# Expert rows by a one-hot product and in two bounded gathers: a decoder step on one core

## What is computed

```python
s = sigmoid(xt @ router_w)                    # 576 x 16 scores
# best of 4 groups by the sum of its two best scores, then the two best experts in that group
w = take(s, e_idx); w = w / sum(w)            # combine: 576 x 16, two entries a row
for e in range(N_EXPERTS):                    # 16 experts, D_EXPERT 512
    h = silu(xt @ e_wg[e]) * (xt @ e_wu[e])
    y = y + combine[:, e:e + 1] * (h @ e_wd[e])
x = layer_norm(DN_ALPHA * x + y, ln_g[2], ln_b[2])
```

## Time and profile before

| | us |
|---|---|
| median of 3 runs | 1470.54 |
| lowest, highest | 1467.07, 1470.69 |
| the profiled execution, its own time | 1473.95 |
| its span, first to last instruction | 1471.7 |

### The profile page before, as it was taken

One profiled execution on the slowest core, in us unless ns is written; L12 is line 12 of the kernel. 1 busy time (PEld: TensorE's weight loads), 2 busy tenths in 40 slices (PEclk: granted clock), 3 DMA queues, 4 the chain that ended last, 5 costly groups with the idle time before them and its releaser, 6 DMA issues.

```text
span 1471.7 us, 20300 instructions
## 1 busy us (share of the span) xinstructions
PE 1338.8 (91%) x8065; PEld 1170.1 (80%) x8065; DVE 788.7 (54%) x1068; ACT 535.5 (36%) x734; POOL 403.3 (27%) x306
## 2 busy tenths in 40 slices
PE   4997998989999888999999999887994999999985
PEld 4987998989888777989998877765883788888862
DVE  7137275572726577722321430322446799999936
ACT  1243421526221454111001011343103688788840
POOL 8464555545245233223332000011000000011010
PEclk9998999999999999999999999997995999999998
DMA  7553323322133212234336301246523899999933
GB/s 242 162 187 102 108 85 111 108 82 86 45 94 87 63 46 65 65 93 119 103 108 201 122 29 57 87 181 241 213 86 95 322 406 410 410 411 412 408 141 128
DMA packets 153498, 239.95 MB, mean 163 GB/s; under 512 B 6400, under 2 KB 111033, under 8 KB 145089
## 3 DMA queue, kind: packets, MB, share of 16 engines
q1 hardware_dynamic: 131472, 177.98, 34.6%
q0 software_dynamic: 14544, 51.52, 9.9%
q10 hardware_dynamic: 7393, 9.20, 1.9%
HBM read 214.08 MB, written 24.60 MB: 162 GB/s over the span
## 4 chain that ended last, share of the span: by engine, by line
PE 49%; DMA 3%; DVE 3%; issue 1%; ACT 1%; POOL 0%; DVEq 0%; POOLq 0%; SPq 0%; ACTq 0%
PE bank L1110 46%; DMA kv_k<-in_cache_mem_k_dram 2%; PE bank L1552 1%; PE bank L1437 1%; PE bank L1135 1%; DVE x_tok L2271 0%; PE bank L1560 0%; DMA yb<-expert_rows,ints 0%; DVE small L2261 0%; ACT kv_t L773 0%; DMA kv_v<-in_cache_mem_v_dram 0%; DMA xg<-x_scratch,table 0%; ACT pT L773 0%; DMA expert_rows<-y_out 0%; DVE expert_weights_lo L2045 0%
## 5 line engine op out<-in xcount | busy, mean ns | idle before, releaser
L2045 DVE TENSOR_TENSOR expert_weights_lo<-expert_weights,expert_weights_hi 128x2048 fp32r<-128x2048 f32 x96 | 218.5, 2290 | 34.5 <-ACT expert_weights_hi L1034 33.2
L1034 ACT ACTIVATE expert_weights_hi<-expert_weights 128x2048 fp32r<-128x2048 f32 x96 | 182.7, 1916 | 22.1 <-PE bank L1110 14.6
L1110 PE MATMUL bank<-x_hi,gate_weights_hi 128*128 128x288 f32 x512 | 163.8, 320 | 12.1 <-ACT gate L932 11.4
L1110 PE MATMUL bank<-x_hi,gate_weights_lo 128*128 128x288 f32 x512 | 152.2, 297 | 0.0
L1110 PE MATMUL bank<-x_lo,gate_weights_hi 128*128 128x288 f32 x512 | 152.1, 297 | 0.0
L1110 PE MATMUL bank<-x_hi,mixer_weights_hi 128*128 128x288 f32 x448 | 137.9, 308 | 0.9 <-ACT q_all L813 0.9
L1110 PE MATMUL bank<-ob,branch_weights 128*128 128x288 f32 (+1 forms) x512 | 134.5, 405 | 0.0
L1110 PE MATMUL bank<-x_lo,mixer_weights_hi 128*128 128x288 f32 x448 | 134.5, 300 | 0.0
L1110 PE MATMUL bank<-x_hi,mixer_weights_lo 128*128 128x288 f32 x448 | 134.3, 300 | 0.0
L2326 POOL TENSOR_TENSOR mixer_weights_lo<-mixer_weights,mixer_weights_hi 128x1024 fp32r<-128x1024 f32 x52 | 128.2, 2466 | 4.2
L932 ACT ACTIVATE gate<-bank,pc 128x288 f32<-128x288 f32 x64 | 31.7, 501 | 226.4 <-PE bank L1110 223.8
(11 more groups left out here) (418 smaller groups left out, 2914.9 us busy)
## 6 DMA issues: line engine op xcount, KB each, us to landing
expert_weights<-in_e_wg_dram SPq DMA_DIRECT2D x32, 1024.0 KB, 8.8
expert_weights<-in_e_wu_dram SPq DMA_DIRECT2D x32, 1024.0 KB, 9.1
expert_weights<-in_e_wd_dram SPq DMA_DIRECT2D x32, 1024.0 KB, 8.9
mixer_weights<-in_w_in_dram SPq DMA_DIRECT2D x36, 512.0 KB, 4.0
gate_weights<-in_w_in_dram SPq DMA_DIRECT2D x32, 512.0 KB, 4.1
branch_weights<-in_w_branch_dram SPq DMA_DIRECT2D x32, 256.0 KB, 3.7
kv_k<-in_cache_mem_k_dram POOLq DMA_DIRECT2D x8, 1024.0 KB, 7.5
kv_v<-in_cache_mem_v_dram POOLq DMA_DIRECT2D x8, 1024.0 KB, 5.5
```

The lines of the kernel that those rows point to most:

```text
L1034: act.activation(w_hi[n % HIS][:], w_raw[n % RAW][:], ACT.Copy).then_inc(w_hi_done, 1)
L1110: return pe.matmul(out, lhsT, rhs, start=start, stop=stop)
L2045: dve.tensor_tensor(w_lo[n % RAW][:], w_raw[n % RAW][:], w_hi[n % HIS][:].bitcast(F32), ALU.subtract).then_inc(w_lo_done, 1)
```

## The change

It has three parts.

**First expert.** Expert 0's turned rows come from a product of x_tok with a one-hot table on PE and no longer from a gather and turns. DVE builds the table first_hot (128 x 640) from the count product, ahead of the slot arithmetic. PE runs 2 x 4 x 5 f32 products of 128 x 128 before it waits for hot_row. On DVE, piece 2's low part moves from ahead of the slot arithmetic to behind the table; x0's low part (`rows_lo(0)`) moves from behind piece 3 to ahead of the table copy. POOL's first gathers are for experts 1 and 2.

**Two passes.** POOL gathers ya and yb twice, with a bound: rows of the first 14 experts (FIRST_PASS, 1792 rows) when expert 13's rows are stored, and the rest after expert 14's (yb) and expert 15's (ya) store. Indices outside a pass lie above its bound, which skips them. The ya tiles lie in other places, free earlier. Expert 15's rows are stored in two halves, each when its half is copied.

**Token rows.** ACT scales x_tok by ALPHA in place in the d steps of experts 0 to 4. DVE adds wb * yb to x_tok after both yb passes (`earlier_term`). PE's sum has then two products for each half, x_tok with the identity and ya with its diagonal, in the order first_terms 0, 1, 2, ya 0, first_terms 3, ya 1, 2, 3, first_terms 4, ya 4. The pair diagonals on DVE are one a tile instead of two and one.

```diff
@@ -477,9 +477,10 @@
-        ya = place("ya", 0, [P, NT, D])
+        ya = [place(f"ya{t}", at, [P, D]) for t, at in enumerate((49088, 50112, 51136, 11264, 40640))]
...
+        first_hot = place("first_hot", 14336, [P, NT, P])
@@ -629,6 +631,8 @@
+        rows_scaled, terms_added = sem("token_rows_scaled"), sem("earlier_terms_added")
+        FIRST_PASS = P * (NE - 2)
@@ -728,8 +732,14 @@
                     store_rows(pieces[before][1])
-            for e in range(NE - 3, NE):
+            for e in range(NE - 3, NE - 1):
                 store_rows(e)
+            e = NE - 1
+            for s, name in enumerate((f"eY{e}", f"eY'{e}")):
+                b, use = uses[name]
+                sp.wait_ge(free[b], use + 1)
+                half = slice(512 * s, 512 * s + 512)
+                sp.dma_start(ys_d[P * e:P * e + P, half], y_out[:, e % 2, half]).then_inc(ys_stored[e % 2], 16)
@@ -1068,6 +1078,10 @@
                         gated(0)
+                    if kind == "d" and part and e < NT:
+                        act.wait_ge(x2_stored, 16 * NT)
+                        rows = x_tok[0:TILES[e], e, :]
+                        act.activation(rows, rows, ACT.Copy, scale=ALPHA).then_inc(rows_scaled, 1)
                     if kind == "d":
@@ -1536,6 +1550,15 @@
+            pe.wait_ge(first_ready, 1)
+            for s in range(2):
+                ps, fu = acquire(pe, f"eX{chr(39) * s}0")
+                for a in range(4):
+                    for t in range(NT):
+                        rows = TILES[t]
+                        m = mm(ps[:, P * a:P * a + P], x_tok[0:rows, t, 4 * s + a:D:KD], first_hot[0:rows, t, :], t == 0, t == NT - 1)
+                m.then_inc(fu, 1)
             pe.wait_ge(hot_ready, 1)
@@ -1562,8 +1585,9 @@
                 if what == "x":
-                    pe.wait_ge(xg_landed[n % 2], 16 * (n // 2 + 1))
-                    turn_gathered(n, n % 2)
+                    if n:
+                        pe.wait_ge(xg_landed[n % 2], 16 * ((n + 1) // 2))
+                        turn_gathered(n, n % 2)
                 elif what == "h":
@@ -1612,35 +1636,32 @@
-                for t in range(NT):
-                    pe.wait_ge(yb_landed[t], 32)
-            pe.wait_ge(diag_ready, NT)
-            def scaled(t, s, n, rows_of_pair, start, stop):
+            def summed(t, s, weights, rows_of_pair, start, stop):
...
-                return mm(bank[sum_banks[t][s]][0:rows, :], pair_diag[0:rows, n, 0:rows],
+                return mm(bank[sum_banks[t][s]][0:rows, :], weights[0:rows, 0:rows],
...
-            def earlier_terms(t):
+            def first_terms(t):
...
-                pe.wait_ge(yb_landed[t], 16)
+                pe.wait_ge(terms_added, t + 1)
...
-                    scaled(t, s, 0, x_tok[:, t, :], True, False)
-                    scaled(t, s, 2 + 2 * t, yb[t][:], False, False)
-            for t in range(NT - 1):
-                earlier_terms(t)
+                    summed(t, s, cst[:, C_ID:C_ID + P], x_tok[:, t, :], True, False)
+            for t in range(3):
+                first_terms(t)
+            pe.wait_ge(diag_ready, NT)
...
-                    earlier_terms(t)
-                pe.wait_ge(ya_landed[t], 16)
+                    first_terms(t)
+                pe.wait_ge(ya_landed[t], 32)
...
-                    scaled(t, s, 1 + 2 * t, ya[:, t, :], False, True).then_inc(sum_full, 1)
+                    summed(t, s, pair_diag[:, t, :], ya[t][:], False, True).then_inc(sum_full, 1)
+                if t == 0:
+                    first_terms(3)
@@ -2138,9 +2159,13 @@
-            weights_lo(2)
             ps, fr = arrived(dve, "pos")
             placed, count = by(ps[:, 0:NT * NE], NE), ps[:, NT * NE:NT * NE + NE]
+            q = col["rest"][:, 0:NT]
+            link(dve.scalar_tensor_tensor(q, placed[:, :, 0], 1.0, by(arr["chosen"], NE)[:, :, 0], ALU.add, ALU.mult))
+            link(dve.tensor_scalar(q, q, -float(P), None, ALU.add))
+            dve.tensor_tensor(first_hot[:], q.unsqueeze(2).to_broadcast([P, NT, P]),
+                              places[:].unsqueeze(1).to_broadcast([P, NT, P]), ALU.is_equal).then_inc(first_ready, 1)
             tiles, ends, starts = (rsc[:, 10, NE * k:NE * k + NE] for k in range(1, 4))
@@ -2173,8 +2198,18 @@
                               places[:].unsqueeze(1).to_broadcast([P, 2 * NT, P]), ALU.is_equal).then_inc(hot_ready, 1)
+            def rows_lo(n):
+                for s in range(2):
+                    ps, fr = arrived(dve, f"eX{chr(39) * s}{n}")
+                    dve.wait_ge(x_hi_out, 2 * n + s + 1)
+                    dve.tensor_tensor(xgT_lo[:, 4 * s:4 * s + 4, :], ps[:, :].rearrange("p (a b) -> p a b", a=4),
+                                      xgT_hi[:, 4 * s:4 * s + 4, :].bitcast(F32), ALU.subtract).then_inc(fr, 1)
+            rows_lo(0)
             ps, fr = arrived(dve, "tab")
             dve.tensor_copy(table[:, 0:MOE_T], ps[:, 0:MOE_T]).then_inc(fr, 1)
+            weights_lo(2)
@@ -2198,7 +2233,6 @@
             dve.tensor_copy(ints[:, 0, 0:NT], slots[:, 0:NT])
-            dve.tensor_scalar(ints[:, 2, 0:NT], slots[:, NT:], float(P * (NE - 1) - 1), None, ALU.min)
             dve.tensor_copy(ints[:, 1, 0:NT], slots[:, NT:]).then_inc(rt_slots, 1)
@@ -2220,17 +2254,15 @@
+                            dve.tensor_scalar(pair_diag[:, e, :], ident, col["wa"][:, e:e + 1], None, ALU.mult).then_inc(diag_ready, 1)
...
-                                dve.tensor_scalar(pair_diag[:, 0, :], ident, ALPHA, None, ALU.mult)
-                            dve.tensor_scalar(pair_diag[:, 1 + 2 * e, :], ident, col["wa"][:, e:e + 1], None, ALU.mult)
-                            dve.tensor_scalar(pair_diag[:, 2 + 2 * e, :], ident, col["wb"][:, e:e + 1], None,
-                                              ALU.mult).then_inc(diag_ready, 1)
+                                link(dve.tensor_scalar(slot_tiles[:], slots[:], float(FIRST_PASS), float(P * 4 * NE), ALU.is_lt, ALU.mult))
+                                link(dve.tensor_tensor(slots[:], slots[:], slot_tiles[:], ALU.add))
+                                dve.tensor_copy(ints[:, 2, 0:NT], slots[:, 0:NT])
+                                dve.tensor_copy(ints[:, 3, 0:NT], slots[:, NT:]).then_inc(rt_slots, 1)
...
-                    for s in range(2):
-                        ps, fr = arrived(dve, f"eX{chr(39) * s}{n}")
-                        dve.wait_ge(x_hi_out, 2 * n + s + 1)
-                        dve.tensor_tensor(xgT_lo[:, 4 * s:4 * s + 4, :], ps[:, :].rearrange("p (a b) -> p a b", a=4),
-                                          xgT_hi[:, 4 * s:4 * s + 4, :].bitcast(F32), ALU.subtract).then_inc(fr, 1)
+                    if n:
+                        rows_lo(n)
@@ -2250,7 +2282,18 @@
                     dve.sem_inc(passed, 1)
+                for t in range(NT):
+                    dve.wait_ge(yb_landed[t], 48)
+            def earlier_term(t):
+                rows = TILES[t]
+                dve.wait_ge(yb_landed[t], 32)
+                x = tile_of(t)
+                dve.scalar_tensor_tensor(x, yb[t][0:rows, :], col["wb"][0:rows, t:t + 1], x, ALU.mult, ALU.add).then_inc(terms_added, 1)
+            dve.wait_ge(rows_scaled, NT)
+            for t in range(NT):
+                earlier_term(t)
             dve.wait_ge(ld_rows, 144)
@@ -2467,23 +2510,37 @@
-            for e in range(2):
-                gather(e, e).then_inc(xg_landed[e], 16)
+            for e in (1, 2):
+                gather(e, e % 2).then_inc(xg_landed[e % 2], 16)
...
-                if what == "x" and n + 2 < NE:
+                if what == "x" and 0 < n < NE - 2:
...
-            def gather_pairs(t, y, k, source):
+            def gather_pairs(t, y, k, end):
...
-                return pool.indirect_dma_start(y[0:rows, :], None, source, bass.IndirectOffsetOnAxis(ap=ints[0:rows, k, t:t + 1], axis=0))
-            pool.wait_ge(rt_slots, 1)
+                return pool.indirect_dma_start(y[0:rows, :], None, ys_d[0:end], bass.IndirectOffsetOnAxis(ap=ints[0:rows, k, t:t + 1], axis=0),
+                                               bounds_check=end - 1, oob_is_err=False)
+            ALL = P * MOE_T
+            pool.wait_ge(rt_slots, 2)
+            pool.wait_ge(ys_stored[0], 16 * (NE // 2 - 1))
+            pool.wait_ge(ys_stored[1], 16 * (NE // 2 - 1))
+            for t in range(4):
+                gather_pairs(t, yb[t], 1, FIRST_PASS).then_inc(yb_landed[t], 16)
+            for t in (4, 3):
+                gather_pairs(t, ya[t], 0, FIRST_PASS).then_inc(ya_landed[t], 16)
+            piece_used(pool, pieces.index(("g", NE - 1, 0)))
+            gather_pairs(4, yb[4], 1, FIRST_PASS).then_inc(yb_landed[4], 16)
+            gather_pairs(0, ya[0], 0, FIRST_PASS).then_inc(ya_landed[0], 16)
+            piece_used(pool, pieces.index(("g", NE - 1, 1)))
+            for t in (1, 2):
+                gather_pairs(t, ya[t], 0, FIRST_PASS).then_inc(ya_landed[t], 16)
...
```

(16 more changed lines are left out.)

## The result

The changed kernel takes 1481.64 us (1479.72 to 1484.8, 4 runs) against 1469.62 (1467.07 to 1470.69, 4 runs) of the kernel before on the same chip: a ratio of 1.008, with a 95% interval of 1.0062 to 1.0098. It is slower by 12 us, where 6.6 less were forecast. The profiled execution took 1479.72 with a span of 1477.6.

The account below looks back on a forecast made before the run. PE was taken as the bound, busy 1338.8 of 1471.7 us, so only its rests could give time. Start 0.6 plus end 6.0 gave 6.6 off 1470.54: 1463.9 us, own range 1461 to 1467, overall range 1460.0 to 1470.5.

Parts of the forecast that it names:

- Product, 11.8 us: At the start, PE's 80 one-hot instructions: 19 at half clock in 4.6 us, the other 61 in 7.2 us.
- the rival at 19.0 us and 1471.1: The one-hot product stays at half clock, 19.0 us instead of 11.8; the start loses 6.6 us; chance 0.06.
- Half clock for 3.2 to 6.0 us of work: After each rest PE runs at 1.2 GHz for this much work; 4.6 us was taken.
- Behind the product, DVE is late and PE rests 7 us: Ahead of expert 1's g step, DVE's full list makes PE rest 7 us instead of 3.3.
- the term of 0.6 us: Gain at the start: g1 comes 1.1 us earlier, less 0.5 for longer half clock; range -0.8 to +2.0.
- POOL's first gathers, 4.6 later, harmless: At the start, expert 1's rows are wanted near 1140 and land by 1135, despite gathers starting 4.6 us later.
- Bounded gathers at the price of plain ones: In POOL's pass one, a bounded gather costs 1.60 us beside DVE and 0.94 plus a gap alone.
- The slower rival: Bounded gathers cost POOL twice, pass one ends at 1430.7, kernel 3.6 us slower at 1474.1; chance 0.11.
- Store of expert 14, 4.5: At the end, expert 14's store among pass one's gathers takes 4.5 us, landing at 1421.9.
- its rival at 7.9: Expert 14's store waits behind pass one for 7.9 us; gain only 3.2 us, 1467.3; chance 0.18.
- Sums to the first statistics, and 1.7 given back: At the end, first_terms 3 between ya 0 and ya 1 delays DVE's statistics, costing 1.7 us of the gain.
- The gain of 6.0 at the end: Behind expert 14: ya 0's first load comes 7.7 us earlier, less 1.7 us given back.

Follow-up runs that it names:

- e9: The changed kernel with 128 adjacent columns of x_tok, not every eighth, as weights of the one-hot product (expert 0's rows permuted): 1466.9 us in one run.
- e13: The same kernel as e9, timed over 10 runs: 1471.02 us, ratio 1.0004 to the kernel before.
- e4: The changed kernel with 512 columns of the one-hot table, not 128, as moving operand of each product (expert 0's rows wrong): the product took 40.89 us.
- e7: The changed kernel with the one-hot table stationary and 512 adjacent x_tok columns moving; ACT copies the rows, PE turns them: 1465.54 us in one run.
- e8: e7 with DVE's pairs' arithmetic moved from ahead of piece 3 to behind piece 8's low part: 1466.91 us, ratio 0.9981 to the kernel before.
- e6: The changed kernel with the one-hot product of one token tile of five (8 products, not 40): expert 0 starts 12.25 us after chosen_r.
- e1: The changed kernel without its first-expert part: two passes, scaled rows and new sums, with the start of the kernel before: 1467.7 us, ratio 0.9996.
- e11: The kernel before with unread products of constants put into PE's waits: 1466.83 us, ratio 0.9981.
- e10: e1 with the first gather pass one expert earlier, bounded at expert 12's rows: 1466.03 us, ratio 0.9981 to the kernel before.
- e12: e10 with unread products of constants put into PE's waits: 1461.82 us, ratio 0.9945 to the kernel before.
- e2: The kernel before with the first-expert part alone (one-hot product and moved DVE steps), its end unchanged: 1480.35 us, ratio 1.0075.
- e3: The changed kernel with x_tok columns, not the one-hot table, as moving operand, so no zeros (expert 0's rows wrong): the product took 23.90 us.

## Why the prediction was wrong, step by step

**Product, 11.8 us: wrong, 23.9.** This is the step that failed. The sum was off by 18.6 us (6.6 faster forecast, 12.0 slower measured); this term is 12.1 of them, and most of the rest is the end, below. The price of 0.119 came from attention products, whose weights lie side by side; the stationary operand here takes every eighth column. Its load takes 0.336 at either clock and can't hide behind 128 columns: 0.243 an instruction, 19.4 us. The 64-row products add 4.5. The stride isn't all of it: adjacent columns still took 15.0 and 16.4 (e9, e13), 3 to 5 more than 11.8, by the 64-row tiles and a later clock. A row of before could have warned: the table product, ten instructions of 24 columns, took 2.63 us, 0.26 each, so a product's price there was not its columns'. The text weighed only whether the clock would return (the rival at 19.0 us and 1471.1, with a chance of 0.06), and doubled or didn't double a price that doesn't follow the clock. That rival named the symptom. Its reason, that every longer stretch had brought the clock back within 6.0 us, failed too: 24 us of unbroken work did not.

**Half clock for 3.2 to 6.0 us of work: too narrow.** It was 3.0 with 512 moving columns (e4, e7), 5.5 in e8, 6.4 and 9.5 in the product from adjacent columns (e9, e13), and in the changed kernel the clock did not return in all of the 23.9. Ahead of expert 1 and in the sums the changed kernel had 3.9 and 3.8, inside the range.

**first_hot and the slot arithmetic: right.** The product starts 3.25 after chosen_r; the forecast had 1115.7, 3.1 after it.

**Behind the product, DVE is late and PE rests 7 us: right in kind.** The rest was 6.1, released by x1's low part, and e6 shows the list to be the limit. What the term of 0.6 us assumed was a product of 11.8; each microsecond more went straight into the g step: 49.3 after chosen_r against the 36.1 of the forecast, 13.2 later for 12.1 of product.

**POOL's first gathers, 4.6 later, harmless: right**, though they came 18 us later; what PE waited for ahead of expert 1 was x1's low part on DVE.

**Nothing inside the loop: right.** 267.2 against 266.9 us; ACT's five scalings took 1.04 to 1.05 each, for the 1.0 of the text.

**Bounded gathers at the price of plain ones: right at rest, low beside DVE.** 0.99 at rest, where a plain one takes 0.94, but 1.9 to 2.6 for the three beside DVE's splits, where the text had 1.6 and had named a bounded gather well over 1.6 as a sign of being wrong. Whether the bound costs this isn't shown. The slower rival, twice the price throughout, did not happen. Ten gathers took from 1416.74 to 1433.3, 16.6 us for the 15.3 of the text.

**Store of expert 14, 4.5: 5.6**, between the forecast and its rival at 7.9. In e1 it was 4.9. The sums start 12.9 after the copy, where the text had 11.7.

**Sums to the first statistics, and 1.7 given back: right.** 8.3 us against 9.05; from the first statistics to the end it is 24.87 against 23.2, the 1.7 of the text.

**The gain of 6.0 at the end: mis-sized, 0.6 by timing, about 3 by profiles.** Its steps held in the main, but they were set against one execution whose clock had been low for 6 of the 18.7 us. Two others of that code had 2.9 and none. The reference of the sum was an unlucky one, and that the profile's 5.6 comes near the 6.0 is luck of the same kind.

## What to carry to other kernels

A product of few columns can be paced by its weight load, so take the price from a row with the same stride in the same operand, and look at the load's row as well as the product's; where the data allow it, let the strided tensor be the moving one, in long adjacent rows (23.9 became 10.9 us here, and expert 0 started 11 us sooner, the copies and turns behind it included). When a step of a chain is replaced, count what else is due at the same time: taking 4 us from DVE's list gave about 1 (e8), because ACT and PE were level with it. A stretch that follows a rest of PE should be read in two or three profiles before its length enters a sum. Where such rests can't be avoided, a few unread products in them gave as much (e11, 0.9981) as the early end did (e10, 0.9981), and both together 0.9945 (e12).

## What the runs showed of the hardware

A weight load of 128 x 128 f32 that takes every eighth column, 32 bytes apart, took 0.312 to 0.338 us at 1.2 and at 2.4 GHz; from adjacent columns it took 0.192 at 2.4 GHz. Behind 512 columns the stride cost nothing: at full clock e4's instructions with it start 0.43 us apart, and so do e7's without. The Trainium skill says why such a load may be slow (SBUF — State Buffer, Door 1: The DMA port swizzle, and Advanced Engine Details and Errata, SBUF Cachelines): SBUF has lines of 16 bytes, an access that goes to a new line each time is penalised, and up to 4 f32 can be strided over for free. The tile views agree with it, and the pages give no size; weighed ahead of the result, it would have spoken against the product's price. The turns of the changed kernel agree too, at a smaller size. Those of gathered rows take every eighth column, those of hidden rows (hs) adjacent ones, both at full clock:

```profile
L1575 PEld LDWEIGHTS bank<-cst,xg x120: 185/192/196, 1153.6 to 1405.6; 128*128 128x128 f32 x120
```

```profile
L1583 PEld LDWEIGHTS bank<-cst,hs x64: 138/139/143, 1168.3 to 1428.3; 128*128 128x128 f32 x64
```

So 0.192 with the stride stands against 0.139 without it for a turn, and 0.336 against 0.192 for a product at full clock. That the strided rows, and not the identity (cst), are what is loaded in a turn is my reading: the identity is the same in both.

Loads of 64 rows between loads of 128 had a rest of 0.22 us before and behind them at 1.2 GHz, also from adjacent columns. At 2.4 GHz in e13 the weight loads stood idle for 0.52 of 4.00 us among such tiles.

The clock stayed at 1.2 GHz through 24 us in which PE was never idle by the profile, in three profiles (the changed kernel, e2, e3), and returned after 3.0 us of 512-column products. Zeros in the operand made no difference (23.88 and 23.90).

A 512 KB store took 2.6 us alone, and 4.9, 5.6 and 6.0 beside gathers (e1, the changed kernel, e10); over all profiles with the new end 4.5 to 6.3.
